# Rounded products of 384 and 192 columns for a hybrid decoder layer's second half of expert scores, and a reordered end

## Chip, core and metric

The kernel runs on one core of one Trainium2 chip. The metric is the device time of one launch in microseconds. Before the change it was 1906.36 us, the median of 3 runs (1906.03 to 1906.52).

## What is computed

One decoder layer on 256 tokens of width 2048, all in float32. A combined input projection feeds a retention group and a sparse attention group, whose joined output is projected and added to the residual. Then comes PEER, a layer of 16384 experts, and a final RMSNorm. PEER is what the change is about:

```python
def peer_ffn(x, wq, subkeys, u, v):
    ...
    def chunk(args):
        xc, ec, gc = args
        hid = jax.nn.gelu(jnp.einsum('cd,chkd->chk', xc, u[ec]))
        return jnp.einsum('chk,chkd->cd', gc * hid, v[ec])
    ...
    return out.reshape(B, T, D)
```

Each token has 128 chosen experts (8 heads of 16) with gates. `u` and `v` have 16384 rows of 2048.

## The kernel before

The program is one hand-written stream of instructions per engine, tied by semaphores. PE multiplies, ACT rounds and evaluates, DVE takes remainders and adds, POOL fetches rows by index, SP loads weight tiles.

**Dense and by pairs.** The first 192 tokens (`TD`) take the dense way: all 16384 experts are computed, in 128 blocks of 128 experts, and multiplied by a gate matrix that is zero for the experts not chosen. The last 64 tokens (`TS`) take only their own experts: 64 u items and 64 v items, each a gather of 128 rows of 8 KB by POOL (`fetch`, line 496) and one pass of DVE over them (`pair_item`, line 1535; lines 1554 and 1557). Between two items nothing but their place in DVE's stream sets the order: `STAGE_ITEMS` tells how many stand in which stretch of blocks, and POOL fetches `GATHER_LEAD` = 3 blocks ahead, into four buffers (`buffer_of`).

**Four stages.** The 128 blocks are worked in two halves of 64. A half has a u stage and a v stage.
- u stage (`u_block`, line 804): a tile of u, 128 x 2048, is loaded by SP into one of four slots of `raw`. PE multiplies its 16 slices of 128 columns by the 16 slices of `xn` (192 tokens), in full float32, line 813, into bank 0 or 1. ACT takes the gelu (line 1150) into `hidden`.
- v stage (`v_block`, line 890): a tile of v is split in two: ACT rounds it to `fp32r` in `hi` (line 1182, halves of 1024 columns), DVE takes the remainder in `lo` (line 1700). The gated hidden values are split likewise into `wm` (lines 1227, 1704, 1705). PE forms 20 products of 512 columns per block (lines 903 to 910) that add up in all eight banks: banks 0 to 3 for tokens 0 to 127, banks 4 to 7 for the other 64, whose rounded part and remainder are packed in one weight tile.
- In the second u stage banks 0 and 1 are wanted for u. So all eight banks are copied to `kept` by ACT (line 1232), stored to memory by POOL, and read back at the end.

In the first v stage the residual is added after the fourth block, by products with the identity: lines 941 (128 columns) and 943 (64 columns) in turn. At the end the 64 pair tokens (`acc`) and the two parts of tokens 128 to 191 are folded together by products with `fold_high` and `fold_low` (lines 956, 957), then come squares, sums, the root and the scaling (lines 1241, 1724, 983 to 985, 1728) in two tiles of 128 tokens.

**What waits for what in the second u stage.** PE's block waits for the tile's load and the gelu before last. SP's next load waits for PE's block. DVE works on pair items alone there. In the v stages SP's load waits for DVE's remainder, ACT's rounding for PE's use of the block two before (`hi` and `lo` have two buffers), DVE for ACT, PE for both.

## Time and profile before

| | us |
|---|---|
| median of 3 runs | 1906.36 |
| the profiled execution's own time | 1907.51 |
| its span, first to last instruction | 1905.7 |
| PE busy | 1872.8 (98%) |
| DVE busy | 1203.8 (63%) |
| ACT busy | 631.8 (33%) |
| DMA, mean | 279 GB/s |
| granted TensorE clock | 0.994 of full |

A group's mean is the time of one instruction from start to end. Products overlap, so the price of one is the time from one start to the next. A full float32 product shows as two instructions, a rounded one (`fp32r`) as one; the views print both as f32. The tables by stage give busy times of each engine in a stretch, with the count of instructions.

### The profile page before, as it was taken

Reading aid. Unit: us, or ns where it says so; the run is one execution under the profiler, and the core shown is the slowest. Engines: PE = TensorE matmul, PEld = TensorE weight load, DVE = VectorE, ACT = ScalarE, POOL = GpSimd, SP = SyncE. Lnnn points to the kernel's source line nnn. Section 1 sums busy time; section 2 is a strip of 40 time slices with the busy share of each in tenths; the row PEclk is TensorE's granted clock in tenths of the full one; section 3 lists DMA queues with packets and bytes.
Section 4 is the critical chain, followed back from the end, with each engine's and each line's share of the span. In section 5 each row is a group of like instructions: output and inputs, shape, how many; then the busy total and the mean of one; then the engine's idle time right before and its main releaser. Section 6 shows DMA issues by size and latency. Waiting matters only on the chain.

```text
span 1905.7 us, 29101 instructions
## 1 busy us (share of the span) xinstructions
PE 1872.8 (98%) x11564; PEld 1702.1 (89%) x11564; DVE 1203.8 (63%) x1929; ACT 631.8 (33%) x906; POOL 228.5 (12%) x151
## 2 busy tenths in 40 slices
PE   8999999998999999999999999999999999999997
PEld 8989999898999999999977777789999998777775
DVE  5535665566339696888457788844232225888885
ACT  5233445454331101111135555520000003555554
POOL 0000000000000111222101131312111112201400
PEclk9999999999999999999999999999999999999999
DMA  8774343455544898989879989879888988999884
GB/s 264 275 273 148 133 136 131 177 177 182 179 147 155 310 335 303 335 332 334 349 298 350 330 312 335 334 304 398 338 339 338 347 313 324 343 350 341 327 310 164
DMA packets 76144, 532.21 MB, mean 279 GB/s; under 512 B 8964, under 2 KB 9220, under 8 KB 15261
## 3 DMA queue, kind: packets, MB, share of 16 engines
q1 hardware_dynamic: 53280, 379.42, 54.0%
q0 software_dynamic: 22400, 151.07, 21.4%
q8 instruction: 52, 0.85, 0.2%
q10 hardware_dynamic: 380, 0.61, 0.1%
q14 instruction: 32, 0.25, 0.0%
HBM read 513.70 MB, written 17.30 MB: 279 GB/s over the span
## 4 chain that ended last, share of the span: by engine, by line
PE 98%; DVE 1%; ACT 0%; issue 0%; DMA 0%; DVEq 0%; ACTq 0%
PE bank L813 35%; PE bank L538 8%; PE bank L539 8%; PE bank L540 8%; PE bank L909 6%; PE bank L904 6%; PE bank L910 6%; PE bank L903 6%; PE bank L908 6%; PE bank L868 2%; PE bank L578 1%; PE bank L616 0%; PE bank L827 0%; PE bank L669 0%; PE bank L688 0%
## 5 line engine op out<-in xcount | busy, mean ns | idle before, releaser
L813 PE MATMUL bank<-hT,raw 128*128 128x192 f32 x4096 | 670.7, 326 | 1.3 <-ACT kept L1232 1.3
L813 PEld LDWEIGHTS bank<-hT,raw 128*128 128x128 f32 x4096 | 665.0, 190 | 2.0 <-issue 2.0
L1700 DVE TENSOR_TENSOR lo<-raw,hi 128x1024 fp32r<-128x1024 f32 x256 | 308.7, 1224 | 117.0 <-ACT hi L1182 116.8
L538 PE MATMUL bank<-act,hi 128*128 128x256 f32 x1216 | 354.3, 291 | 11.4 <-DVE act L1261 6.2
L1182 ACT ACTIVATE hi<-raw 128x1024 fp32r<-128x1024 f32 x256 | 270.6, 1060 | 273.2 <-PE bank L910 268.8
L539 PE MATMUL bank<-act,hi 128*128 128x256 f32 x1216 | 347.3, 286 | 0.0
L540 PE MATMUL bank<-act,lo 128*128 128x256 f32 x1216 | 347.1, 285 | 0.0
L1253 DVE TENSOR_TENSOR lo<-raw,hi 128x2048 fp32r<-128x2048 f32 x76 | 174.1, 2291 | 146.6 <-ACT hi L969 83.5
L538 PEld LDWEIGHTS bank<-act,hi 128*128 128x128 f32 x1216 | 236.5, 195 | 20.5 <-issue 19.2
L1150 ACT ACTIVATE arena<-bank 128x192 f32<-128x192 f32 x128 | 42.3, 330 | 591.4 <-PE bank L813 591.4
L539 PEld LDWEIGHTS bank<-act,hi 128*128 128x128 f32 x1216 | 236.6, 195 | 1.5 <-issue 1.4
L540 PEld LDWEIGHTS bank<-act,lo 128*128 128x128 f32 x1216 | 236.4, 194 | 0.0
L1557 DVE SCALAR_TENSOR_TENSOR acc<-rows_sb,wcol,acc 128x2048 f32<-128x2048 f32 x64 | 150.3, 2349 | 123.9 <-DMA rows_sb<-in_v,pairs 123.5
L1554 DVE SCALAR_TENSOR_TENSOR rows_sb<-rows_sb,xs 128x2048 f32<-128x2048 f32 x64 | 146.5, 2289 | 113.3 <-DMA rows_sb<-in_u_rows,pairs 113.1
L904 PE MATMUL bank<-lo,wm 128*64 128x512 f32 x512 | 202.6, 396 | 0.0
L909 PE MATMUL bank<-hi,wm 128*128 128x512 f32 x512 | 202.4, 395 | 0.0
L903 PE MATMUL bank<-hi,wm 128*128 128x512 f32 x512 | 199.3, 389 | 2.9 <-DVE wm L1705 2.9
L910 PE MATMUL bank<-hi,wm 128*128 128x512 f32 x512 | 200.9, 392 | 0.0
L908 PE MATMUL bank<-lo,wm 128*128 128x512 f32 x512 | 199.6, 390 | 0.0
L503 POOL DMA_INDIRECT rows_sb<-in_v,pairs x64 | 104.0, 1625 | 492.8 <-PE bank L910 186.5
L503 POOL DMA_INDIRECT rows_sb<-in_u_rows,pairs x64 | 105.7, 1651 | 444.5 <-PE bank L910 167.7
L908 PEld LDWEIGHTS bank<-lo,wm 128*128 128x128 f32 x512 | 96.2, 188 | 46.5
(258 smaller groups left out, 1564.6 us busy)
## 6 DMA issues: line engine op xcount, KB each, us to landing
raw<-in_u SPq DMA_DIRECT2D x128, 1024.0 KB, 6.1
raw<-in_v SPq DMA_DIRECT2D x128, 1024.0 KB, 7.3
raw<-in_w_in SPq DMA_DIRECT2D x44, 1024.0 KB, 5.4
raw<-in_w_out SPq DMA_DIRECT2D x16, 1024.0 KB, 5.2
raw<-in_wq SPq DMA_DIRECT2D x16, 1024.0 KB, 4.8
gate_matrix<-gs POOLq DMA_DIRECT2D x12, 768.0 KB, 12.3
gs<-gate_matrix SPq DMA_DIRECT2D x12, 768.0 KB, 9.1
raw<-in_cmp_w SPq DMA_DIRECT2D x8, 1024.0 KB, 4.9
```

Of the source, the lines that this page charges most:

```text
L503: pool.indirect_dma_start(rows_sb[b][:, :], None, (u_rows, v_rows)[kind == "v"], bass.IndirectOffsetOnAxis(ap=pair_rows[:, j:j + 1], axis= ...
L538: mm(dst, wh, mh, start=first, stop=False)
L539: mm(dst, wh, ml, start=False, stop=False)
L540: return mm(dst, wl, mh, start=False, stop=last)
L813: last = mm(bank[s % 2][:, 0:TD], raw[:, s, k * P:(k + 1) * P], xn[:, k, 0:TD], start=(k == 0), stop=(k == KT - 1))
L903: mm(bank[4 + dc][:, :], packed, vh[:, cols], start=opening, stop=False, skip_group_check=True)
L904: return mm(bank[4 + dc][0:TS, :], packed[:, 0:TS], vl[:, cols], start=False, stop=closing, skip_group_check=True)
L908: mm(bank[dc][:, :], whole, vl[:, cols], start=opening, stop=False, skip_group_check=True)
L909: mm(bank[dc][:, :], whole, vh[:, cols], start=False, stop=False, skip_group_check=True)
L910: return mm(bank[dc][:, :], rest, vh[:, cols], start=False, stop=closing, skip_group_check=True)
L1182: do(hi[:, s % 2, cols], raw[:, s, cols], ACT.Copy).then_inc(v_hi_ready, 1)
L1700: vec.tensor_tensor(lo[:, mv % 2, cols], raw[:, mv % RAW, cols], hi[:, mv % 2, cols].bitcast(F32), ALU.subtract).then_inc(v_lo_ready, 1)
```

## The change

- **Second u stage.** The tiles of u in the second half are split by ACT and DVE as those of v (`round_split`, `rest_split`), and `xn` too, into `xr`: 192 rounded columns and 192 of remainder per slice. A slice of 16 then takes two rounded products: `hi` by all 384 columns and `lo` by the 192 rounded ones (`REST_COLS`). They replace one full float32 product. Rounded times remainder stands in the bank's second 192 columns, so DVE adds the two (`sum_u`) and ACT's gelu works on the sum (`hidden_gelu`). The remainder of u times that of xn is left out, as it is in the v stages.
- `xr` is made in the first v stage, blocks 24 to 40, one slice a block on ACT and DVE (`spread_xn`, `spread_rest`). It takes the place of `xn` and of one gather buffer; from there on three buffers are used. `STAGE_ITEMS` has 27, 38 and 25 items for 26, 42 and 22.
- **Between the halves** banks 2 to 7 keep adding up through both halves; only banks 0 and 1 are copied (`kept`). Nothing goes to memory and back.
- **v blocks** form the products of tokens 128 to 191 of half a tile before those of tokens 0 to 127.
- **Residual.** All steps with 128 columns stand first, then those with 64 columns, alternately into the two halves of the banks' partitions.
- **End.** The pair tokens are finished by themselves during the last v blocks (POOL adds them with a DMA, ACT and DVE scale them). In the last block the products of tokens 128 to 191 come first, are copied by ACT and DVE and folded into 64 + 64 partitions by four products (`fold_second_tiles`) ahead of banks 2 and 3. One table of functions is loaded ahead for the logarithm and the exponential.

```diff
-def v_halves(half): return 2 * HALF * half
+SPLIT_0 = m_v(0)
+SPREAD_AT = 24
+REST_COLS = 192
...
-STAGE_ITEMS = ((PAIRS_LISTED, ROUTED, FIRST_GATHERS), (ROUTED, HALF - 4, 24), (HALF, 2 * HALF, 26),
-               (2 * HALF, 3 * HALF - 3, 42), (3 * HALF, 4 * HALF - 10, 22))
+STAGE_ITEMS = ((PAIRS_LISTED, ROUTED, FIRST_GATHERS), (ROUTED, HALF - 4, 24), (HALF, 2 * HALF, 27),
+               (2 * HALF, 3 * HALF - 3, 38), (3 * HALF, 4 * HALF - 10, 25))
...
-    return i % 2 if i < FIRST_GATHERS else 2 + i % 2 if items_by(HALF + 8) > i else i % 4
+    return i % 2 if i < FIRST_GATHERS else 2 + i % 2 if items_by(HALF + 8) > i else (0, 2, 3)[i % 3]
...
-        kept_back = at("kept_back", 40960, [P, 2 * D])
+        xr = at("xr", 22528, [P, KT, 2 * TD], F32R)
...
+        kept = [gs[:, x, 1536:2048] for x in range(2)]
...
+                if half:
+                    with sp.Fori(0, HALF // RAW) as lap:
+                        for s in range(RAW):
+                            load_after_v(a["u"][RAW * lap + (HALF + s)], 2 * RAW * lap + 2 * (HALF - RAW + s + 1), s)
...
+            def u_split_block(r, s, opening=False):
+
+                if opening:
+                    pe.wait_ge(half_kept, r + 1)
+                    pe.wait_ge(xr_lo, KT)
+                else:
+                    pe.wait_ge(u_summed, r - 1)
+                acc_bank = bank[s % 2]
+                for k in range(KT):
+                    if k % 8 == 0:
+                        pe.wait_ge(v_hi_ready, 2 * r + (2 * HALF + k // 8 + 1))
+                        pe.wait_ge(v_lo_ready, 2 * r + (2 * HALF + k // 8 + 1))
+                    w = slice(k * P, (k + 1) * P)
+                    mm(acc_bank[:, 0:2 * TD], hi[:, s % 2, w], xr[:, k, :], start=(k == 0), stop=False, skip_group_check=True)
+                    last = mm(acc_bank[:, 0:REST_COLS], lo[:, s % 2, w], xr[:, k, 0:REST_COLS], start=False, stop=(k == KT - 1),
+                              skip_group_check=True)
+                    if k == 7:
+                        last.then_inc(v_half_done, 1)
+                last.then_inc(block_done, 1)
+
...
+                        for part in range(2):
+                            split_loaded(part)
+                            for dc in (2 * part, 2 * part + 1):
+                                second_tile(dc)
+                            if opening and part == 0:
+                                if half:
+                                    pe.wait_ge(u_summed, HALF)
+                                else:
+                                    pe.wait_ge(acc_evacuated, M_PEER + HALF)
+                            for dc in (2 * part, 2 * part + 1):
+                                last = first_tile(dc)
+                                if closing and dc == 0:
+                                    last.then_inc(sums_done, 1)
+                            if part == 0:
                                 last.then_inc(v_half_done, 1)
                     last.then_inc(block_done, 1)
 
-
-                pe.wait_ge(acc_evacuated, M_PEER + HALF * (half + 1))
...
+                def fold_second_tiles():
+
+                    for dc in range(4):
+                        if dc % 2 == 0:
+                            pe.wait_ge(fold_even, dc // 2 + 1)
+                            pe.wait_ge(fold_odd, dc // 2 + 1)
+                        last = mm(bank[4 + dc // 2][TS * (dc % 2):TS * (dc % 2 + 1), :], fold_rows, fold_in[:, dc * 512:(dc + 1) * 512],
+                                  start=True, stop=True)
+                    last.then_inc(folded, 1)
...
-                            last = mm(bank[4 + dc][0:TS, j * P:(j + 1) * P], res_back[:, k * T + P:k * T + TD],
+                    for dc in range(4):
+                        for j in range(4):
+                            k, x = 4 * dc + j, j % 2
+                            last = mm(bank[4 + dc][TS * x:TS * (x + 1), j * P:(j + 1) * P], res_back[:, k * T + P:k * T + TD],
                                       ident, start=False, stop=False, skip_group_check=True)
...
+            def hidden_gelu(r):
+
+                ac.wait_ge(u_summed, r + 1)
+                cols = hidden[:, r * TD:(r + 1) * TD]
+                do(cols, cols, ACT.Gelu_apprx_tanh).then_inc(acc_evacuated, 1)
...
+            def round_split(n):
+
+                s, m = n % RAW, SPLIT_0 + n
+                ac.wait_ge(raw_loaded[s], 16 * ((m + 8) // RAW + 1))
                 for part in range(2):
...
-                    if part == 0 and mv >= 2:
-                        ac.wait_ge(v_half_done, (HALF - 1) * half + mv - 1)
+                    if part == 0 and n >= 2:
+                        ac.wait_ge(v_half_done, n - 1)
                     else:
-                        ac.wait_ge(block_done, m_v(half) + mv - 1)
...
+            def spread_xn(k):
+
+                if k == 0:
+                    ac.wait_ge(res_added, 1)
+                    ac.wait_ge(wm_lo, SPREAD_AT - 1)
+                if k >= 5:
+                    ac.wait_ge(xr_lo, min(k, math.ceil(1.5 * k - 6.5)))
+                src = xn_last[:, k - KT + 2, :] if k >= KT - 2 else xn[:, k, 0:TD]
+                do(xr[:, k, 0:TD], src, ACT.Copy).then_inc(xr_hi, 1)
...
+            def round_gated(half, mv):
+
+                weights = hidden[:, mv * TD:(mv + 1) * TD]
...
-                    for r in range(HALF):
-                        if r == HALF - 1:
-                            round_v(1, 0)
-                        hidden_block(1, r)
+                    for r in range(1, HALF):
+                        round_split(HALF + r)
+                        if r >= 2:
+                            hidden_gelu(r - 2)
...
+                    if half and mv == HALF - 6:
+
+                        nc.scalar.preload_act_table_set("natural_log_exp_and_others")
+                        ac.wait_ge(acc_folded, 16)
+                        do(squares[0:TS, 0:D], fin_third, ACT.Square, accum_out=small[0:TS, 8:9]).then_inc(fin_sq, 1)
+                        ac.wait_ge(fin_sq, 1)
+                        rsqrt(small[0:TS, 8:9], small[0:TS, 9:10], D, fin_log, fin_rstd, 1, rows=TS)
-                    ac.wait_ge(block_done, m_v(0) + HALF)
-                    for b in range(8):
-                        do(kept[:, b * 512:(b + 1) * 512], bank[b][:, :], ACT.Copy).then_inc(half_kept, 1)
...
+                    round_split(HALF)
+                    for x in range(2):
+                        if x == 0:
+                            ac.wait_ge(sums_done, 1)
+                        else:
+                            ac.wait_ge(v_half_done, HALF)
+                        do(kept[x], bank[x][:, :], ACT.Copy).then_inc(half_kept, 1)
...
+            def rest_split(n, part):
+
+                cols = slice(part * 1024, (part + 1) * 1024)
+                dv.wait_ge(v_hi_ready, 2 * n + part + 1)
+                vec.tensor_tensor(lo[:, n % 2, cols], raw[:, n % RAW, cols], hi[:, n % 2, cols].bitcast(F32),
+                                  ALU.subtract).then_inc(v_lo_ready, 1)
+
+            def sum_u(r):
+
+                dv.wait_ge(block_done, m_u(1) + r + 1)
+                vec.tensor_reduce(hidden[:, r * TD:(r + 1) * TD], bank[r % 2][:, 0:2 * TD].rearrange("p (a t) -> p t a", a=2),
+                                  AX.X, ALU.add).then_inc(u_summed, 1)
+
+            def spread_rest(k):
+
+                src = xn_last[:, k - KT + 2, :] if k >= KT - 2 else xn[:, k, 0:TD]
+                dv.wait_ge(xr_hi, k + 1)
+                vec.tensor_tensor(xr[:, k, TD:2 * TD], src, xr[:, k, 0:TD].bitcast(F32), ALU.subtract).then_inc(xr_lo, 1)
+
             for half in range(2):
                 if half:
-                    items_to(items_by(3 * HALF - 1))
-                    dv.wait_ge(half_stored, 16)
+                    for r in range(HALF):
+                        rest_split(HALF + r, 0)
+                        if r >= 2:
+                            sum_u(r - 2)
+                        rest_split(HALF + r, 1)
+                        items_to(items_by(2 * HALF + r - 1))
 
                 for mv in range(HALF):
...
+                    rest_split(2 * HALF * half + mv, 0)
+                    if half and mv < 2:
+                        sum_u(HALF - 2 + mv)
+                    rest_split(2 * HALF * half + mv, 1)
+                    if half == 0 and mv == SPREAD_AT - 2:
+                        for k in range(2):
+                            vec.tensor_copy(xn_last[:, k, :], xn[:, KT - 2 + k, 0:TD])
+                    if half == 0 and 0 <= mv - SPREAD_AT - 1 < KT:
+                        spread_rest(mv - SPREAD_AT - 1)
...
+            dv.wait_ge(fin_rstd, 1)
+            vec.scalar_tensor_tensor(out=fin_third, in0=fin_third, scalar=small[0:TS, 9:10], in1=norm_row[0:TS, :],
+                                     op0=ALU.mult, op1=ALU.mult).then_inc(fin_ready, 1)
+            for dc in (1, 3):
+                dv.wait_ge(sums_done, dc + 2)
+                vec.tensor_copy(fold_in[:, dc * 512:(dc + 1) * 512], bank[4 + dc][:, :]).then_inc(fold_odd, 1)
+            for dc in range(2):
+                dv.wait_ge(sums_done, dc + 6)
+                vec.tensor_tensor(fin_first[:, dc * 512:(dc + 1) * 512], bank[dc][:, :], kept[dc], ALU.add).then_inc(fin_added, 1)
```

**PE, from the last products of the first v stage to the second u stage.** `hT` holds `xn`. Before:

```order
L910 MATMUL bank<-hi,wm 128x512
L908 MATMUL bank<-lo,wm 128x512
L909 MATMUL bank<-hi,wm 128x512
L910 MATMUL bank<-hi,wm 128x512
L813 MATMUL bank<-hT,raw 128x192 x64
```

With the change:

```order
L935 MATMUL bank<-hi,wm 128x512
L933 MATMUL bank<-lo,wm 128x512
L934 MATMUL bank<-hi,wm 128x512
L935 MATMUL bank<-hi,wm 128x512
L835 MATMUL bank<-xr,hi 128x384
L836 MATMUL bank<-xr,lo 128x192
L835 MATMUL bank<-xr,hi 128x384
L836 MATMUL bank<-xr,lo 128x192
```

One kind of product of 192 columns, 16 a block, has become two kinds in turn, 16 of each.

**DVE, early in the second u stage.** Lines 1557 and 1554 (before) and 1648 and 1645 (now) are pair items. Before:

```order
L1557 SCALAR_TENSOR_TENSOR acc<-rows_sb_63,wcol,acc 128x2048 [waits rows_fetched3,acc_step]
L1554 SCALAR_TENSOR_TENSOR rows_sb_60,hcol<-rows_sb_60,xs 128x2048 [waits rows_fetched0]
L1554 SCALAR_TENSOR_TENSOR rows_sb_61,hcol<-rows_sb_61,xs 128x2048 [waits rows_fetched1]
L1554 SCALAR_TENSOR_TENSOR rows_sb_62,hcol<-rows_sb_62,xs 128x2048 [waits rows_fetched2]
L1554 SCALAR_TENSOR_TENSOR rows_sb_63,hcol<-rows_sb_63,xs 128x2048 [waits rows_fetched3]
L1547 TENSOR_TENSOR wcol<-hcol,pairs 128x4 [waits hcol_ready]
L1557 SCALAR_TENSOR_TENSOR acc<-rows_sb_60,wcol,acc 128x2048 [waits acc_step,rows_fetched0,acc_begun,wcol_ready]
L1557 SCALAR_TENSOR_TENSOR acc<-rows_sb_61,wcol,acc 128x2048 [waits rows_fetched1,acc_step]
L1694 TENSOR_TENSOR wmt<-arena,gs 128x192 [waits wm_lo,acc_evacuated,gate_loaded0,half_stored]
L1700 TENSOR_TENSOR lo<-raw,hi 128x1024 [waits v_hi_ready] x2
```

With the change:

```order
L1773 TENSOR_TENSOR lo<-raw,hi 128x1024 [waits v_hi_ready]
L1779 TENSOR_REDUCE arena<-bank 128x192 [waits block_done]
L1773 TENSOR_TENSOR lo<-raw,hi 128x1024 [waits v_hi_ready] x2
L1779 TENSOR_REDUCE arena<-bank 128x192 [waits block_done]
L1773 TENSOR_TENSOR lo<-raw,hi 128x1024 [waits v_hi_ready]
L1648 SCALAR_TENSOR_TENSOR acc<-rows_sb_59,wcol,acc 128x2048 [waits rows_fetched0,acc_step]
L1773 TENSOR_TENSOR lo<-raw,hi 128x1024 [waits v_hi_ready]
L1779 TENSOR_REDUCE arena<-bank 128x192 [waits block_done]
L1773 TENSOR_TENSOR lo<-raw,hi 128x1024 [waits v_hi_ready]
L1648 SCALAR_TENSOR_TENSOR acc<-rows_sb_61,wcol,acc 128x2048 [waits rows_fetched2,acc_step]
```

Items that stood in a row now stand between the remainders of u (line 1773) and the sums (line 1779), both of which PE waits for.

**PE, the residual after the fourth v block.** Before:

```order
L908 MATMUL bank<-lo,wm 128x512
L909 MATMUL bank<-hi,wm 128x512
L910 MATMUL bank<-hi,wm 128x512
L941 MATMUL bank<-base,res_back 128x128
L943 MATMUL bank<-base,res_back 64x128
L941 MATMUL bank<-base,res_back 128x128
L943 MATMUL bank<-base,res_back 64x128
```

With the change:

```order
L933 MATMUL bank<-lo,wm 128x512
L934 MATMUL bank<-hi,wm 128x512
L935 MATMUL bank<-hi,wm 128x512
L984 MATMUL bank<-base,res_back 128x128 x16
L989 MATMUL bank<-base,res_back 64x128 x16
L992 UNCONDITIONAL_BRANCH
```

The steps with 128 and with 64 columns of weights no longer alternate.

## Rows read from the trace of the kernel before

**Rows 1.** Page, part 4: share of the span in the chain that ended last.
```profile
PE 98%; DVE 1%; ACT 0%; issue 0%; DMA 0%; DVEq 0%; ACTq 0%
PE bank L813 35%; PE bank L538 8%; PE bank L539 8%; PE bank L540 8%; PE bank L909 6%; PE bank L904 6%; PE bank L910 6%; PE bank L903 6%; PE bank L908 6%; PE bank L868 2%; PE bank L578 1%; PE bank L616 0%; PE bank L827 0%; PE bank L669 0%; PE bank L688 0%
```

**Rows 2.** Busy time by stage: first v, second u, second v.
```profile
core 0: us, PE busy (x) PEld busy (x) DVE busy (x) ACT busy (x) POOL busy (x), PEclk, DMA share, GB/s
...
950.00:1257.00 307.00, 307.00 (x1340) 233.46 (x1339) 243.56 (x328) 148.13 (x191) 56.96 (x24) 1.00 0.89 324
1259.00:1593.00 334.00, 333.04 (x2048) 332.77 (x2048) 100.99 (x70) 26.96 (x81) 49.76 (x45) 1.00 0.88 342
1594.00:1889.00 295.00, 295.00 (x1280) 226.35 (x1280) 251.88 (x354) 148.95 (x193) 53.94 (x20) 1.00 0.86 321
```

**Rows 3.** Groups by line and shape, whole span (busy us, mean ns of one).
```profile
L1700 DVE TENSOR_TENSOR lo<-raw,hi 128x1024 fp32r<-128x1024 f32 x256 | 308.7, 1224 | 117.0 <-ACT hi L1182 116.8
L1182 ACT ACTIVATE hi<-raw 128x1024 fp32r<-128x1024 f32 x256 | 270.6, 1060 | 273.2 <-PE bank L910 268.8 <-DMA raw<-in_v 4.4
L1150 ACT ACTIVATE arena<-bank 128x192 f32<-128x192 f32 x128 | 42.3, 330 | 591.4 <-PE bank L813 591.4
L1557 DVE SCALAR_TENSOR_TENSOR acc<-rows_sb,wcol,acc 128x2048 f32<-128x2048 f32 x64 | 150.3, 2349 | 123.9 <-DMA rows_sb<-in_v,pairs 123.5
L1694 DVE TENSOR_TENSOR wmt<-arena,gs 128x192 f32<-128x192 f32 x96 | 52.4, 546 | 17.6 <-DMA gs<-gate_matrix 17.6
L1400 DVE SCALAR_TENSOR_TENSOR hT<-bank,gs 128x384 f32<-128x384 f32 x16 | 8.9, 557 | 3.3 <-PE bank L669 3.3
```

**Rows 4.** Chain that ended last, in order of time: start us, us, what.
```profile
562.34 7.14 PE bank L827 x64
...
578.53 3.65 PE bank L836 x64
...
968.64 0.36 PE bank L943 x2
969.01 0.42 PE bank L941 x2
...
1259.35 333.05 PE bank L813 x2048
```

**Rows 5.** Timeline of PE, two w_q products 24 apart, two L903 five apart, the last ones.
```profile
470.71 0.28 PE L539 MATMUL bank<-act,hi 128*128 128x256 f32 x1
...
473.57 0.28 PE L539 MATMUL bank<-act,hi 128*128 128x256 f32 x1
...
1882.14 0.39 PE L903 MATMUL bank<-hi,wm 128*128 128x512 f32 x1
...
1883.29 0.39 PE L903 MATMUL bank<-hi,wm 128*128 128x512 f32 x1
...
1888.79 0.39 PE L910 MATMUL bank<-hi,wm 128*128 128x512 f32 x1
```

**Rows 6.** Second u stage (1259 to 1593 us) in 40 slices: rate of all DMA.
```profile
GB/s 188 378 427 422 421 421 420 423 289 379 307 325 367 276 396 279 410 398 276 348 334 308 375 281 408 274 403 379 283 345 318 333 377 286 409 390 175 263 234 340
```

**Rows 7.** Waits of DVE in the same stage: us in total, times, longest us.
```profile
DVE acc L1557 <- DMA rows_sb<-in_v,pairs: 117.8, 22, 21.6
```

**Rows 8.** Timeline of PE, the first product of the stages (idle before it <- releaser).
```profile
949.75 0.47 PE L903 MATMUL bank<-hi,wm 128*128 128x512 f32 x1 [1.44 <-DVE wm L1705]
...
1259.35 0.40 PE L813 MATMUL bank<-hT,raw 128*128 128x192 f32 x1 [1.27 <-ACT kept L1232]
...
1593.82 0.47 PE L903 MATMUL bank<-hi,wm 128*128 128x512 f32 x1 [1.44 <-DVE wm L1705]
```

**Rows 9.** Timeline of the end of the kernel.
```profile
1896.09 0.60 ACT L1241 ACTIVATE arena<-bank 128x512 f32<-128x512 f32 x1 [0.35 <-PE bank L957]
...
1899.69 0.20 ACT L985 ACTIVATE small<-small 128x1 f32<-128x1 f32 x1
1899.93 2.73 DVE L1728 SCALAR_TENSOR_TENSOR arena<-bank,small,hT 128x512 f32<-128x512 f32 x4 [2.96 <-ACT small L985]
```

250 lines of the change are left out of this document (120 added, 130 removed).

## The prediction

> **What bounds the kernel now.** I read the chain that ended last first: 98% of the span is TensorE, 35% of it on line 813, the full float32 products of both u stages [rows 1]. So the time is what PE has to do, as long as its operands are there, and every price below is a time from one PE start to the next. The table by stage says the same for the two v stages and the second u stage: PE is busy in practically all of each [rows 2]. The reader is to see in it that the engines beside PE are very unlike: DVE is at 79% and 85% in the v stages, but at 30% in the second u stage (100.99 of 334.00 us), and ACT at 8%. The clock there is granted in full (1.00). The chain in order of time then gives the u stage its price: 333.05 us for 64 blocks of 16 products, 1024 in all, so 0.325 us a product of 192 columns [rows 4]. PE's timeline gives the price of a rounded product (one instruction each): 24 of 256 columns from 470.71 to 473.57, so 0.119 us; five of 512 columns from 1882.14 to 1883.29, so 0.230 us [rows 5].
>
> The sum is made against the profiled execution's own 1907.51 us (span 1905.7); the median of the runs shown is 1906.36, 1.15 less, which I take off at the end.
>
> **The u stage, PE.** Of 1024 products at 0.325 us become 1024 of 384 columns and 1024 of 192, all rounded. The first lies between two measured sizes: the line through 256 and 512 columns rises 0.111 us in 256 columns, so 384 cost 0.119 + 0.0555 = 0.1745 us. No rounded product under 256 columns stands in this trace, so the second is bounded from both sides. Below: the same line drawn on, 0.119 - 0.028 = 0.091 us. Above: the full float32 price of the same 192 columns, 0.325 us. I take neither. A product of 192 columns is so short that loading its 128 columns of weights may take longer. The nearest row for that is line 827, 64 instructions with loads of 128 columns in 7.14 us, 0.1116 each; with loads of 64 columns into alternating halves (line 836) the same count takes 3.65 us [rows 4]. So 0.1116 us, since the only thing in the new product unlike the 256-column one is its width, and nothing in the rows makes a rounded product dearer when it is narrower. Per weight tile 0.1745 + 0.1116 = 0.286 us, times 1024 = 293 us: **40.2 us less** than 333.05.
>
> The Trainium skill states another rule, in "TensorE: Matmul & The Clock Gate", section "Back-to-back issue gap": a product follows the last after its columns over 2.4 GHz plus 2.5 ns. The trace disagrees at both widths it has, 216 ns by the Trainium skill against 230 [rows 5] for 512 columns and 109 against 119 for 256. By the Trainium skill alone the pair would be 162.5 + 82.5 = 245 ns and PE's share of the stage 251 us. What that would make of the time is the rival of the unburdened narrow product below.
>
> **The u stage, what must now keep up.** The stage's u tiles are now rounded by ACT and the remainder taken by DVE, as in the v stages, and DVE adds the two halves of a bank before ACT's gelu.
> - DVE per block: two remainders, 308.7/256 = 1.206 us each [rows 3], 2.41; the sum, which reads 384 columns from a bank, at least 0.33 (ACT's copy-like pass over 192) and at most about 0.7 (half as much again as the nearest); I take the nearest row, line 1400 with 384 columns from a bank, 0.557; and 38 pair items in 64 blocks at 2.35 [rows 3], 1.40. Together 4.37 us, 280 us for the stage, beside PE's 4.58 and 293. That is 95% and the closest cover in this forecast. If PE were faster than 280 us, DVE would hold it.
> - ACT per block: two roundings at 1.06 and a gelu at 0.33 [rows 3], 2.45 us of 4.58. Costs nothing.
> - The rounded and remainder tiles have two buffers each. ACT may start a block's first half only when PE has used half of the block two before. So a remainder may come 1.5 blocks, 6.9 us, after its buffer is free; it takes 1.06 + 1.21, and at most one item (2.35) and one sum (0.56) stand ahead of it: 5.2 us. It fits, without much room. Nothing queued on ACT behind the new wait for the sum is late by more than the sum itself.
> - DMA: 64 tiles and 38 gathers of 1.05 MB are 107 MB (now 64 and 42, in 333 us). In 293 us that is 365 GB/s. The stage runs at 342 now [rows 2], but slices of it at 421 to 427 [rows 6], so the rate exists. SP's loads now wait for the remainder and not for PE's block; the remainder comes earlier, so a load is issued no later.
>
> **The v stages.** In the first, 16 slices of xn are rounded by ACT and their remainders taken by DVE: 16 x 0.33 = 5.3 us on ACT, 18 x 0.546 = 9.8 us [rows 3] and one item more, 2.35, on DVE. It goes from 243.6 to about 256 of 307 us [rows 2]: covered. In the second, three items more (7 us) on 251.9 of 295: covered. If that cover were gone, all of it, some 19 us, would be on the path. Gathers have three buffers for four; POOL fetches about 4.5 blocks ahead, an item comes every 1.6 blocks or more, so a buffer is free when the fetch is due. The second tile's products stand ahead of the first tile's; that moves nothing in the sum, since PE issues the same 20 per block.
>
> **Adding the residual.** Now each 128-column step is followed by a 64-column one on line 943: 0.36 + 0.42 us a pair [rows 4], 16 such pairs, 12.5 us. Afterwards all of line 941's kind come first, 32 instructions at 0.1116 (line 827), and then 32 with 64-column loads that alternate between two halves, as line 836's do, 3.65/64 = 0.057 us. 3.6 + 1.8 = 5.4 us: **7.1 us less**. Unless the residual's layout, and not the alternation, makes these steps slow; then nothing.
>
> **Three joints.** PE stood 1.27 us for ACT's copy of a bank between the halves and 1.44 us for DVE's wm before each v stage, at 949.75 and 1593.82 [rows 8]. Afterwards a bank's copy begins while the last v block still runs, only two banks are copied, and a v block opens with products that need no u result. 1.27 + 2 x 1.44 = **4.1 us less**.
>
> **The end.** Now the last product starts at 1888.79 [rows 5] and the span ends at 1905.7, 16.9 us. The 64 pair tokens are finished before, and the half sums are not brought back. What stays behind the last product: its 0.39, a square 0.8 with its read, a sum 0.2 and two small steps of 0.2 to 0.3 each with their hand-overs, 0.8, scaling four 512-wide pieces 2.73, two more 1.4 [rows 9], and the last DMA, which now takes the 3.0 us from 1902.7 to the end. That is 9.4 us, 7.5 less, also because one table for both small steps is loaded ahead. Against it stand four folding products ahead of the last six: between 1.7 us, if their halves run beside each other, and 3.4; I take 2.5. **5.0 us less**. The new waits of the fold, on ACT's and DVE's copies of 0.6 to 0.7 us, lie under six products of 0.23.
>
> **Sum.** 1907.5 - 40.2 - 7.1 - 4.1 - 5.0 = 1851.1, less 1.15: **1850 us**.
>
> **Rivals.**
> - *The narrow product keeps its full float32 price* (ends slower). For it: the trace has no rounded product under 256 columns, while all 192-column products of the u stages cost 0.325; if the array gives the rounded rate only from some width on, the narrow product pays this. Against it: between 512 and 256 columns the price falls nearly in step with the width. Pair 0.1745 + 0.325 = 0.500 us, stage 512 us, 179 more: 1907.5 + 178.6 - 16.2 - 1.2 = 2069. It decides from a narrow product of 0.167 us on: there the pair costs 0.341 and the stage's loss of 16 us eats the 16.2 gained elsewhere. DVE would idle, with 8.0 us a block to fill.
> - *Half of that*: one float32 instruction of the two, 0.163. Stage 345, 12 more: 1902, not to be told from no change.
> - *DVE's waits for gathers take the stage.* Now DVE stands up to 21.6 us for a gather in this stage, 117.8 us in all for line 1557's [rows 7], at no cost, since nothing PE needs is behind it. Now remainders are. If the loads and gathers keep to the stage's 342 GB/s, its 107 MB take 313 us: 20 less than now and not 40, 1870. Against: most of those waits come from DVE running ahead of the fetches, which items now placed after each block can't.
> - *The narrow product isn't held by its weights* (the rule of the Trainium skill is one form of it). At 0.091 PE needs 272 us, under DVE's 280, which then holds: 1907.5 - 53 - 16.2 - 1.2 = 1837.
> - That the change doesn't do what it says is no rival: the order of PE's instructions shows both widths alternating.
>
> **Chances.** The forecast 0.56; narrow product unheld 0.13; gather waits 0.13; float32 price 0.15; half of it 0.03. A measurement of this kernel tells 0.2% (3.8 us) from no change. Faster by more: 0.82; within: 0.03; slower: 0.15. The range takes in the rivals at 1837 and 1870 with the bounds of their costs (the residual's 7 us either way, DVE's sum at 0.33 to 0.7, 10 us a side): 1828 to 1880. It leaves out the float32 price and its half, 0.18.
>
> **What would show it.** In the profile after: a start-to-start of 0.11 us for the narrow product (line 836 of the changed kernel) beside 0.17 for the wide one (its line 835), a stage of 64 blocks in 293 us with DVE over 90% busy; the residual in 5 to 6 us; no idle over 0.5 us at the joints; 10 us from the last product to the end, the fold aside. Wrong it is if the narrow one's is above 0.15, if DVE's idle in the stage is put down to gathers, or if PE waits for the remainders (its line 1773) block by block.

## The result, and the profile after

The changed kernel takes 1846.12 us, the median of 4 runs (1845.95 to 1846.27); the kernel before took 1906.34 beside it (1906.03 to 1906.52). The ratio is 0.9684, with a 95% interval of 0.9667 to 0.9701. The profiled execution has 1846.27 us and a span of 1844.5, 61.2 us less than before. The mean granted TensorE clock is 0.994 in both.

The page of the kernel after, its span, busy times and chain (as [rows 1]):

```profile
span 1844.5 us, 29701 instructions
...
PE 1815.4 (98%) x11560; PEld 1654.8 (90%) x11560; DVE 1380.4 (75%) x2133; ACT 764.3 (41%) x1043; POOL 162.5 (9%) x151
...
PE 97%; DVE 1%; ACT 0%; issue 0%; DMA 0%; DVEq 0%; ACTq 0%
PE bank L819 18%; PE bank L835 11%; PE bank L548 8%; PE bank L549 8%; PE bank L550 8%; PE bank L929 6%; PE bank L928 6%; PE bank L933 6%; PE bank L934 6%; PE bank L935 6%; PE bank L836 5%; PE bank L894 2%; PE bank L588 1%; PE bank L626 0%; PE bank L853 0%; PE bank L679 0%
```

PE still sets the time. The float32 products, now line 819, have fallen from 35% of the span to 18%; the two rounded ones (835 wide, 836 narrow) take 16%. DVE has gone from 63% to 75%, with nothing of it on the chain to speak of.

The table by stage, for the first v stage, the second u stage and the second v stage (as [rows 2]; stretch, length, busy us and count of PE, PEld, DVE, ACT, POOL, clock, DMA share, GB/s):

```profile
947.00:1246.80 299.80, 298.91 (x1344) 231.27 (x1343) 251.76 (x349) 157.91 (x215) 28.16 (x28) 1.00 0.94 341
1246.90:1538.00 291.10, 291.10 (x2048) 291.10 (x2047) 266.98 (x258) 154.40 (x196) 41.79 (x37) 1.00 0.96 369
1538.00:1834.00 296.00, 295.76 (x1290) 226.62 (x1289) 258.10 (x358) 154.85 (x204) 26.00 (x25) 1.00 0.89 326
```

The second row is the change's heart: 2048 products in 291.10 us, PE never idle, DVE at 92% of it where it had 30%, DMA at 369 GB/s where it had 342. PE's timeline shows the joint to the second u stage and, far inside it, the steady pair (start, us, engine and line; as [rows 5] and [rows 8]):

```profile
1246.67 0.39 PE L935 MATMUL bank<-hi,wm 128*128 128x512 f32 x1
1246.89 0.33 PE L835 MATMUL bank<-xr,hi 128*128 128x384 f32 x1
...
1300.26 0.25 PE L836 MATMUL bank<-xr,lo 128*128 128x192 f32 x1
1300.26 0.19 PEld L835 LDWEIGHTS bank<-xr,hi 128*128 128x128 f32 x1
1300.34 0.36 PE L835 MATMUL bank<-xr,hi 128*128 128x384 f32 x1
1300.37 0.19 PEld L836 LDWEIGHTS bank<-xr,lo 128*128 128x128 f32 x1
1300.54 0.25 PE L836 MATMUL bank<-xr,lo 128*128 128x192 f32 x1
1300.54 0.19 PEld L835 LDWEIGHTS bank<-xr,hi 128*128 128x128 f32 x1
```

The joint is 0.22 us from start to start, a product's usual price. A pair takes 1300.54 - 1300.26 = 0.28 us; over the stage, 291.25/1024 = 0.2844. The recorded starts of the products split it as 0.08 for the narrow one and 0.20 for the wide; the starts of the loads (PEld) split it as 0.11, from the load of line 835 to that of line 836, and 0.17 to the next one of line 835. Which product pays for what the two don't tell alike, and the experiments had to. The other thing to see is when a load starts: the wide product's weights (line 835) begin to load when the narrow one before it starts, no sooner.

The groups that answer to [rows 3], and the passes over gathered rows (as [rows 7]):

```profile
L1773 DVE TENSOR_TENSOR lo<-raw,hi 128x1024 fp32r<-128x1024 f32 x384 | 463.7, 1221 | 113.0 <-ACT hi L1232 112.5
L1232 ACT ACTIVATE hi<-raw 128x1024 fp32r<-128x1024 f32 x384 | 404.8, 1059 | 325.8 <-PE bank L935 236.3 <-PE bank L836 82.9 <-DMA raw<-in_v 6.2
...
L1648 DVE SCALAR_TENSOR_TENSOR acc<-rows_sb,wcol,acc 128x2048 f32<-128x2048 f32 x64 | 150.2, 2347 | 8.9 <-DMA rows_sb<-in_v,pairs 8.3
...
L1779 DVE TENSOR_REDUCE arena<-bank 128x192 f32<-128x384 f32 x64 | 35.2, 550 | 0.0
```

Line 1773 has 384 instructions for 256: a third stage is split. The sum of a bank's halves (1779) takes 0.550 us. DVE's idle before the passes of line 1648 for a gather has gone from 123.5 us to 8.3. The waits inside the second u stage are short (engine and line, waited for: total us, times, longest):

```profile
POOL rows_sb L513 <- DVE acc L1648: 120.2, 19, 8.6
...
ACT hi L1232 <- PE bank L836: 81.7, 88, 1.2
ACT arena L1200 <- DVE arena L1779: 41.2, 44, 2.5
DVE lo L1773 <- ACT hi L1232: 23.8, 47, 1.2
```

PE waits for nothing in this stage, and DVE waits for ACT's rounding alone, by half a microsecond a time. POOL waits for DVE now to free a buffer; DVE never waits for POOL's gathers.

Stage by stage, from the first PE start of one to that of the next, in us:

| | before | after | difference | forecast |
|---|---|---|---|---|
| up to the first u product | 557.0 | 555.5 | -1.4 | 0 |
| first u stage, joint | 392.8 | 391.0 | -1.7 | -1.4 |
| first v stage, joint | 309.6 | 300.3 | -9.3 | -8.4 |
| second u stage, joint | 334.5 | 291.3 | -43.2 | -41.6 |
| second v stage, with the fold | 295.0 | 295.9 | +0.9 | +2.5 |
| last product's start to the end | 16.9 | 10.45 | -6.5 | -7.5 |
| sum (rounded parts) | 1905.7 | 1844.5 | -61.2 | -56.4 |

The chain in order of time shows the residual (as [rows 4]):

```profile
965.19 3.57 PE bank L984 x32
968.76 1.90 PE bank L989 x32
970.66 0.42 PE bank L928
```

3.57 + 1.90 = 5.47 us, where it was 12.5. And the timeline of the end (as [rows 9]; in brackets the idle time before and what ended it):

```profile
1831.81 1.03 PE L972 MATMUL bank<-arena,base 128*64 128x512 f32 x4
...
1834.05 0.39 PE L935 MATMUL bank<-hi,wm 128*128 128x512 f32 x1
...
1834.47 0.60 ACT L1317 ACTIVATE arena<-bank 128x512 f32<-128x512 f32 x1
...
1835.38 0.29 ACT L1027 ACTIVATE small<-small 128x1 f32<-128x1 f32 x1 [0.22 <-DVE small L1838]
1835.71 0.20 ACT L1029 ACTIVATE small<-small 128x1 f32<-128x1 f32 x1
...
1837.12 0.61 PE L1000 MATMUL bank<-small,base 128*128 128x1 f32 x4 [2.69 <-ACT arena L1317]
...
1838.60 1.40 DVE L1846 SCALAR_TENSOR_TENSOR arena<-bank,small,hT 128x512 f32<-128x512 f32 x2
1840.02 1.50 SPq L481 DMA_DIRECT2D out<-arena  x2
```

No loading of a table stands between the two small steps (1027 and 1029). PE's last work is to add up the other tile's squares at 1837.12, and after DVE's last scaling 4.5 us go by to the end of the span.

### The profile page after: what moved, and what is told of

Its sections match the earlier page's. It is cut to its first block, busy times and chain, and to the rows that moved or that the text cites. A ratio compares the mean times of both kernels' runs of the same rounds, so it can differ in the third digit from the quotient of the medians.

```text
span 1844.5 us, 29701 instructions
## 1 busy us (share of the span) xinstructions
PE 1815.4 (98%) x11560; PEld 1654.8 (90%) x11560; DVE 1380.4 (75%) x2133; ACT 764.3 (41%) x1043; POOL 162.5 (9%) x151
## 4 chain that ended last, share of the span: by engine, by line
PE 97%; DVE 1%; ACT 0%; issue 0%; DMA 0%; DVEq 0%; ACTq 0%
PE bank L819 18%; PE bank L835 11%; PE bank L548 8%; PE bank L549 8%; PE bank L550 8%; PE bank L929 6%; PE bank L928 6%; PE bank L933 6%; PE bank L934 6%; PE bank L935 6%; PE bank L836 5%; PE bank L894 2%; PE bank L588 1%; PE bank L626 0%; PE bank L853 0%; PE bank L679 0%
## 5 line engine op out<-in xcount | busy, mean ns | idle before, releaser
L1773 DVE TENSOR_TENSOR lo<-raw,hi 128x1024 fp32r<-128x1024 f32 x384 | 463.7, 1221 | 113.0 <-ACT hi L1232 112.5
L1232 ACT ACTIVATE hi<-raw 128x1024 fp32r<-128x1024 f32 x384 | 404.8, 1059 | 325.8 <-PE bank L935 236.3
L819 PE MATMUL bank<-hT,raw 128*128 128x192 f32 x2048 | 337.6, 326 | 0.0
L819 PEld LDWEIGHTS bank<-hT,raw 128*128 128x128 f32 x2048 | 332.2, 190 | 0.3 <-issue 0.3
L835 PE MATMUL bank<-xr,hi 128*128 128x384 f32 x1024 | 291.3, 359 | 0.0
L836 PE MATMUL bank<-xr,lo 128*128 128x192 f32 x1024 | 256.3, 250 | 0.0
L836 PEld LDWEIGHTS bank<-xr,lo 128*128 128x128 f32 x1024 | 195.6, 191 | 0.0
L835 PEld LDWEIGHTS bank<-xr,hi 128*128 128x128 f32 x1024 | 191.8, 187 | 0.0
```

The lines of the kernel that those rows point to most:

```text
L819: last = mm(bank[s % 2][:, 0:TD], raw[:, s, k * P:(k + 1) * P], xn[:, k, 0:TD], start=(k == 0), stop=(k == KT - 1))
L835: mm(acc_bank[:, 0:2 * TD], hi[:, s % 2, w], xr[:, k, :], start=(k == 0), stop=False, skip_group_check=True)
L836: last = mm(acc_bank[:, 0:REST_COLS], lo[:, s % 2, w], xr[:, k, 0:REST_COLS], start=False, stop=(k == KT - 1), skip_group_check=True)
L1232: do(hi[:, s % 2, cols], raw[:, s, cols], ACT.Copy).then_inc(v_hi_ready, 1)
L1773: vec.tensor_tensor(lo[:, n % 2, cols], raw[:, n % RAW, cols], hi[:, n % 2, cols].bitcast(F32), ALU.subtract).then_inc(v_lo_ready, 1)
```

## The experiments

Each starts from the kernel after and changes what its diff shows. The expectations number the theories. The first is the forecast's own: a narrow product is held to 0.1116 us by a load of 128 weight columns. The others are what speaks against it: that the price follows the width, or that a rounded product grows dear below some width. Beside the three groups of runs the kernel before took 1906.78, 1906.54 and 1906.62 us. The first u product starts between 555.2 and 556.3 us in kernels that are alike up to there, so the length of a stage tells more than a total.

### What does the narrow product's price depend on?

**Its width: 256, 128 and 64 columns.** With 128 or 64, the tokens above that number go without the product of u's remainder; with 256, 64 tokens gain the product of both remainders, which the kernel leaves out. The edit for 256, the other two alike:

```
-REST_COLS = 192
+REST_COLS = 256
```

> The changed kernel with narrow products of 256 columns instead of 192; the 64 extra columns add a term of remainder times remainder that is left out otherwise. Measured so far: a pair of wide and narrow product takes 0.285 us, 292 us a stage, 1846.1 us in all. Theory 1, the 192-column product is held by the load of its 128 columns of weights (0.111 us) and costs nothing for its columns: at 256 columns it costs what such products cost in the w_q stage, 0.119, the pair 0.2935, the stage 8.7 us more, 1855 us. Theory 2, the pair is paid by its columns at 0.434 ns each: 28 us more, 1874. Theory 3, narrow products are dear under some width between 192 and 256: the pair gets cheaper or stays.

> The changed kernel with narrow products of 128 columns; this leaves out the product of u's remainder for tokens 128 to 191. Theory 1 (held by the weight load): 0.111 us as before, no change, 1846 us. Theory 2 (paid by columns): 28 us of PE less, PE at 264 us a stage; DVE was busy 267 us in it and would then hold at 270 to 280: 1826 to 1836 us. Theory 3 (narrow products are dear under some width): twice the price of a float32 instruction of 128 columns, 0.223 us, the pair 0.40, 115 us more: 1961.

> The changed kernel with narrow products of 64 columns; this leaves out the product of u's remainder for tokens 64 to 191. Theory 1 (held by the weight load): no change, 1846 us. Theory 2 (paid by columns): PE at 235 us a stage, DVE holds at 270 to 280: 1826 to 1836 us. Theory 3: the pair above 0.29 us, slower than 1850.

Measured: 256 columns 1856.17 us (ratio 0.9735, 0.9719 to 0.9751), stage 300.4; 128 columns 1848.82 (0.9696, 0.968 to 0.9713), stage 293.5; 64 columns 1849.98 (0.9702, two runs only), stage 293.5; and 192, the kernel after, 291.2. So a product of 256 columns costs 9.2/1024 = 0.009 us more than one of 192, about as far as 0.119 is above 0.1116, and below 192 nothing is gained: the pair goes from 0.2844 to 0.2866, slightly up. Below the 0.11 us, whatever sets them, the width is free. That speaks against both other theories at once: if the price followed the width, a product of 64 columns would save 10 to 20 us, as far as DVE lets it; if narrow products grew dear, the pair would take 0.29 us and more. Both kernels are slower than the 1846 us that the weight load alone had them at, by 2.7 and 3.9 us, of which 2.2 lie in this stage. PE's timeline at 256 columns:

```profile
1300.09 0.28 PE L836 MATMUL bank<-xr,lo 128*128 128x256 f32 x1
1300.21 0.34 PE L835 MATMUL bank<-xr,hi 128*128 128x384 f32 x1
1300.38 0.28 PE L836 MATMUL bank<-xr,lo 128*128 128x256 f32 x1
```

0.12 and 0.17: the price of 256 columns and, within the 0.01 us of these starts, the 0.1745 that the forecast's line gives 384; nothing is held. The two prices make 0.2935, and the stage has 300.4/1024 = 0.2934.

**Its own load: 64 weight columns.** Only half of the experts of a tile get their remainder.

```
-                    last = mm(acc_bank[:, 0:REST_COLS], lo[:, s % 2, w], xr[:, k, 0:REST_COLS], start=False, stop=(k == KT - 1),
+                    last = mm(acc_bank[0:TS, 0:REST_COLS], lo[:, s % 2, k * P:k * P + TS], xr[:, k, 0:REST_COLS], start=False, stop=(k == KT - 1),
```

> The changed kernel with narrow products of 192 columns, but with only 64 columns of weights, so that the load is half as long; this leaves out u's remainder for half of the experts of a block. Theory 1 (the 192-column product is held by the load): the load falls to 0.057 us and the product costs its columns, 0.091; the pair 0.266, PE 272 us a stage instead of 292; DVE, busy 267 us there, is nearly the bound: stage 272 to 282 us, 1826 to 1836 us. Theory 2 (not the load): no change, 1846 us.

Measured: 1845.39 us (0.9678, 0.9662 to 0.9694), the stage 290.1 us, 1.1 less than the kernel after. Theory 1, as worded, missed (1826 to 1836): a narrow product with half the load costs practically what it did. Either the load had never held it, and some other floor of 0.11 us did, or the load that holds it is another one. The timeline of the kernel after points to the second: while the narrow product runs, the weights that are being loaded are those of the *next wide* product. The narrow one's own were loaded under the wide one before it, which lasts 0.1745 us and covers them. So the edit had halved a load that was hidden.

**The wide product's load: 64 weight columns.** The counterpart. Half of the experts of a tile get no rounded part of u; the work of every other engine is kept. The edit halves the outputs of the wide product as well as its load; the same halving of the narrow product, just now, brought 1 us.

```
-                    mm(acc_bank[:, 0:2 * TD], hi[:, s % 2, w], xr[:, k, :], start=(k == 0), stop=False, skip_group_check=True)
+                    mm(acc_bank[0:TS, 0:2 * TD], hi[:, s % 2, k * P:k * P + TS], xr[:, k, :], start=(k == 0), stop=False, skip_group_check=True)
```

> The changed kernel with only 64 columns of weights in the wide product (384 columns), the narrow product whole; this leaves out most of the scores of half the experts of a block. Halving the narrow product's own load changed nothing (pair 0.284 us). Theory 1, corrected: a load runs while the product before it runs, so what the narrow product waits out is the load of the next wide product, 128 columns, 0.111 us. Halved it is 0.057, less than the narrow product's 0.091: pair 0.266, PE 272 us a stage; DVE was busy 267 us and nearly holds it: stage 272 to 282 us, 1827 to 1837 us. Rival: the pair has a fixed price of its own that no load sets: no change, 1846 us.

Measured: 1832.98 us (0.9613, 0.9598 to 0.9628), the stage 278 us. PE's timeline:

```profile
1300.03 0.25 PE L836 MATMUL bank<-xr,lo 128*128 128x192 f32 x1
1300.03 0.13 PEld L835 LDWEIGHTS bank<-xr,hi 128*64 128x64 f32 x1
1300.12 0.34 PE L835 MATMUL bank<-xr,hi 128*64 128x384 f32 x1
1300.12 0.19 PEld L836 LDWEIGHTS bank<-xr,lo 128*128 128x128 f32 x1
1300.30 0.25 PE L836 MATMUL bank<-xr,lo 128*128 128x192 f32 x1
```

The row of that stage in the table by stage, and then PE's wait for DVE among the waits:

```profile
1246.80:1524.80 278.00, 274.56 (x2050) 272.83 (x2049) 265.55 (x258) 149.82 (x196) 42.02 (x37) 1.00 0.98 384
```

```profile
PE bank L835 <- DVE arena L1779: 3.2, 5, 1.0
```

A pair now takes 0.27 us (0.266 over five of them), which is 0.1745 + 0.091, the price the forecast gave a narrow product that nothing holds. The same product, with the same weights of its own, costs 0.09 or 0.11 us by what is loaded behind it. This split of the pair is worked out from the price of 384 columns; what is measured is that the pair is 0.018 us shorter. The row of the table shows the next two bounds coming near: DVE is at 96% and DMA's share at 0.98, and PE begins to wait for DVE's sum, 3.2 us in all.

The Trainium skill, in "TensorE: Matmul & The Clock Gate", section "Back-to-back issue gap", gives columns over 2.4 GHz plus 2.5 ns for a product taken by itself, and says that this comes out too low for few columns, because it leaves no time for the weight load. By it the pair would take 245 ns. Neither run agrees: 284 ns with the load in the way and 266 without.

**The order: two wide, then two narrow.** If the loads for both narrow products could be made under the wide ones, or the load of a wide one earlier, the narrow ones would not be held.

```
+                    for j in (k, k + 1):
+                        w = slice(j * P, (j + 1) * P)
+                        mm(acc_bank[:, 0:2 * TD], hi[:, s % 2, w], xr[:, j, :], start=(j == 0), stop=False, skip_group_check=True)
+                    for j in (k, k + 1):
+                        w = slice(j * P, (j + 1) * P)
+                        last = mm(acc_bank[:, 0:REST_COLS], lo[:, s % 2, w], xr[:, j, 0:REST_COLS], start=False, stop=(j == KT - 1),
+                                  skip_group_check=True)
```

> The changed kernel with the products of two slices in the order wide, wide, narrow, narrow. Corrected theory 1 (one load ahead and no more): each narrow product still has a load of 128 columns to wait out, two pairs take 2 x 0.1745 + 2 x 0.111: no change, 1846 us. Rival (loads can run further ahead, and only the turning between widths costs): 20 ns a pair less, PE at 272 us a stage, 1827 to 1837 us.

PE's timeline (838 is the wide product here, 841 the narrow one; a row holds two):

```profile
1300.06 0.36 PE L841 MATMUL bank<-xr,lo 128*128 128x192 f32 x2
1300.26 0.54 PE L838 MATMUL bank<-xr,hi 128*128 128x384 f32 x2
1300.64 0.36 PE L841 MATMUL bank<-xr,lo 128*128 128x192 f32 x2
```

Measured: 1848.65 us (0.9692), the stage 293.5. Two pairs take 1300.64 - 1300.06 = 0.58 us; over the stage a pair takes 0.2866, 0.002 more than in turn, which is not explained, and not 0.02 less. In either order a narrow product has one load of 128 columns behind it and costs 0.11. If loads could be made further ahead, that of the second narrow product would be done under the wide ones, and at least the first narrow one would not be held. So here only one load is made ahead.

### What does DVE's cover amount to?

**The sum three times over** in 60 of the 64 blocks, the two extra results going nowhere.

```
+                if r < HALF - 4:
+                    vec.tensor_reduce(spare[(r + 0) % 3], bank[r % 2][:, 0:2 * TD].rearrange("p (a t) -> p t a", a=2),
+                                  AX.X, ALU.add)
+                    vec.tensor_reduce(spare[(r + 1) % 3], bank[r % 2][:, 0:2 * TD].rearrange("p (a t) -> p t a", a=2),
+                                  AX.X, ALU.add)
```

> The changed kernel with the sum of a bank's halves taken three times by DVE in 60 of the 64 blocks of the second u stage, twice into spare memory. DVE is busy 267 of 291 us there. If that cover is as thin as its busy time says: 60 x 2 x 0.46 to 0.55 us more are 55 to 66, DVE at 322 to 333 us sets the stage, 31 to 42 us more: 1877 to 1888 us. If DVE's work hides at no such limit (PE doesn't wait for it): 1846 us.

A stretch of 322 us inside the stage in the table by stage, and the waits of PE and DVE in it (1786 is the sum here):

```profile
1248.00:1570.00 322.00, 294.51 (x1974) 288.22 (x1974) 310.55 (x364) 140.52 (x187) 40.85 (x36) 0.98 0.89 321
```

```profile
PE bank L835 <- DVE arena L1786: 27.4, 30, 2.4
...
DVE lo L1773 <- ACT hi L1232: 11.3, 27, 1.2
```

Measured: 1888.56 us (0.9903), the stage 333.3 us, 42 more. DVE is busy for 321 us of it, where it was 267: the 120 extra sums are 54 us of busy time, 0.45 each, and not 66, because one starts 0.46 to 0.47 us after the last though it lasts 0.55. Of the 54 us, 12 were covered and 42 are the stage's growth; of DVE's 24 idle microseconds 12 are left, waits for ACT's rounding. So DVE sets the stage at 96% busy, and PE waits for the sum 30 times in some 62 blocks.

The growth is not all waiting: PE waits for 27.4 us. Its four longest waits, 1.87 to 2.42 us (they end at 1312.64, 1381.38, 1446.12 and 1514.87), are followed within 2 us by slices with a granted clock of 0.50, the lower of the clock's two levels. From 1313.92 to 1314.45 a pair takes 0.53 us there instead of 0.284, and the kernel after has 1.00 over the whole stage. How much of the 42 us this makes was not measured by a run of its own.

### What is the rest of the change worth?

**The second u stage in full float32 again**, ACT's roundings, DVE's remainders and sums and the items all kept. DVE's sum reads the one half that is left twice. Because PE reads `raw` again, SP's loads in this stage wait for PE's block, as before, and no longer for DVE's remainder; the lines below are PE's only.

```
-                    mm(acc_bank[:, 0:2 * TD], hi[:, s % 2, w], xr[:, k, :], start=(k == 0), stop=False, skip_group_check=True)
-                    last = mm(acc_bank[:, 0:REST_COLS], lo[:, s % 2, w], xr[:, k, 0:REST_COLS], start=False, stop=(k == KT - 1),
+                    last = mm(acc_bank[:, 0:TD], raw[:, s, w], xr[:, k, 0:TD].bitcast(F32), start=(k == 0), stop=(k == KT - 1),
```

> The changed kernel with one full float32 product of 192 columns in the second u stage instead of the two rounded ones; all else of the change stays, the splitting of u by ACT and DVE and the sum too. The product works on the rounded part of xn and the sum counts it twice, so the hidden values of that half are not those of the reference. If the rounded pair is the whole gain of the stage and the rest of the change is worth the other 18 us: stage 333 instead of 292 us, 1846 + 41 = 1887 us. If the added work of DVE and ACT costs something of its own in the float32 stage: above 1890.

Measured: 1887.56 us (0.99, 0.9884 to 0.9917), the stage 333 us again. The products, with that wait of SP, are worth 41.4 us, everything else 19.

**The residual in turn**, as before: a 128-column step, then a 64-column one, all into the lower half of the partitions.

```
-                            k = 4 * dc + j
+                            k, x = 4 * dc + j, 0
...
-                    for dc in range(4):
-                        for j in range(4):
-                            k, x = 4 * dc + j, j % 2
```

> The changed kernel with the residual's products in the order of before: a step with 128 columns of weights, then one with 64, in turn, the latter always into the lower 64 partitions. If the turning between the two sizes of load is what made these steps slow: they take 12.5 us instead of the 5.5 measured with the change, 7 us more, 1853 us. If not (the residual's layout, or the memory it comes from): they stay at about 5.5, 1846 us.

**The residual grouped, but on one side**: the 64-column steps no longer alternate between halves. The fold adds both halves, so all of it may go into one.

```
-                            k, x = 4 * dc + j, j % 2
+                            k, x = 4 * dc + j, 0
```

> The changed kernel with the residual's products grouped by size, but all 64-column ones into the lower 64 partitions. If alternating halves lets two run beside each other: without it 32 instructions at 0.107 to 0.112 us take 3.5 us instead of 1.9, 1.6 us more, 1847.7 us. If the halves don't matter: 1846.1 us.

The chain in order of time, first in turn (986 has the 64 columns here, 984 the 128), then on one side:

```profile
966.75 0.36 PE bank L986 x2
967.12 0.42 PE bank L984 x2
967.54 0.36 PE bank L986 x2
```

```profile
965.81 3.57 PE bank L984 x32
969.38 3.64 PE bank L989 x32
```

Measured: in turn 1853.8 us (0.9721), first v stage 307.5 us against 300.3; on one side 1849.11 (0.9706; 1848.13 to 1854.1), stage 302.1. In the profiled executions the stage also starts later than in the kernel after, by 1.0 and 0.6 us. Of the 7.1 us that taking turns costs, 5.4 come back by grouping, 1.7 by alternating between halves. With 64 columns of weights into the half that is in use an instruction costs 3.64/32 = 0.114 us, no less than one with 128 (0.1116). So in these steps it is not the weight load that sets 0.11. They are full float32 with 128 columns to multiply by; at line 819's price, 0.325/2 us for 192 columns, those alone make 0.108 us, an estimate.

**No table loaded ahead** for the end.

```
-                        nc.scalar.preload_act_table_set("natural_log_exp_and_others")
```

> The changed kernel without the table load ahead of the end. If the loads were a part of the old end's length: logarithm and exponential load a table each (1.28 us) in both of the last roots, two loads or more on the path, 2.6 to 5.1 us more, 1848.7 to 1851.2 us. If the loads fall into waits: under 1 us more.

The timeline of its end:

```profile
1836.35 1.28 ACT L1027 ACT_TABLE_LOAD   x1
...
1837.96 1.28 ACT L1029 ACT_TABLE_LOAD   x1
...
1840.66 1.01 PE L1000 MATMUL bank<-small,base 128*128 128x1 f32 x4 [5.05 <-ACT arena L1316]
```

Measured: 1851.81 us (0.9713). Two of the four loads of 1.28 us are in the first tile's way, two in the second's. From the last product to the end it is 14.4 us against 10.45; another 1.1 us lie in the second v stage, in front of its last product, where PE waits 1.3 us for ACT's rounding, once. The median is 0.6 us above the upper end of what was expected.

**The last tile's output by two queues.** Stores are issued piece by piece by SP and ACT rather than at the end by SP alone.

```
+            for c in range(2):
+                ac.wait_ge(fin_ready, 6 + c)
+                nc.scalar.dma_start(out[P:P + TS, c * 1024 + 512:(c + 1) * 1024], fin_second[TS:P, c * 512:(c + 1) * 512]).then_inc(out_stored, 16)
```

> The changed kernel with the last rows written in four pieces, each as soon as it is scaled, half of them issued by ACT beside SP. Between DVE's last scaling and the end lie 4.5 us, two transfers issued 0.75 us apart. If the issue and the wait for both pieces are part of it: 0.7 to 1.5 us less, 1844.6 to 1845.4 us. If the last transfer's own time is all: no change, 1846.1 us.

Measured: 1845.56 us (0.9678, 0.9665 to 0.9691), 0.6 less than the kernel after, with ranges that overlap (1845.25 to 1846.26 here, 1845.95 to 1846.27 there). After DVE's last scaling 3.7 us go by to the end instead of 4.5, and from the last product's start 9.7 instead of 10.45. So the stretch that the edit touches is 0.7 us shorter, the low end of what was expected; the total hardly tells it from nothing.

## Why the prediction was right, point by point

The forecast was 1850 us in a range of 1828 to 1880; measured are 1846.1. Of the 4.8 us by which the span fell further than the sum, 1.4 lie ahead of the first u product, where the change has nothing; among the changed kernels that start moves by 1.0 us by itself. The second u stage and the second v stage gave 1.6 us each more than forecast, the end 1.0 less, the first u and the first v stage 1.2 together.

- **The u stage.** Forecast 0.286 us a pair and 293 us, measured 0.2844 and 291.2. Both terms stand: 384 columns at 0.1745, as the run with 256 beside it shows, and a floor of 0.11 for the narrow product, which the widths 64, 128 and 192 show to be no matter of width. Two things in the working of that floor were wrong, and the number came out right by luck. It named the wrong load: it said that a product of 192 columns is so short that loading *its* weights takes longer. It is the load for the product behind it. In this kernel both have 128 columns, so the number was the same; an edit built on the wording, halving the narrow one's load, brought 1 us of the 10 to 20 it seemed to promise, and halving the other one brought 13. And it took 0.1116 from line 827, full float32 products of 128 columns, as the price of a load. Such an instruction costs about as much by its columns (0.108, the estimate above), and costs 0.114 with half the load, as the residual on one side shows. So that row did not tell the two apart; that a load of 128 columns takes 0.11 us is seen in the changed kernel, where the next load starts 0.11 us after it.
- **The other engines keep up.** DVE's single durations add up to about what was forecast (remainders 157, sums 35, items 90 in that stage: 282 for 280), but instructions overlap a little, and it is busy for 267 of 291 us, 92% and not 95%. It is idle for 24 us, of which the three sums a block could use 12. Remainders, waited for by PE block by block, had been named as a sign that the working is wrong; there is no such wait.
- **The gathers' rival** (1870) fell: DMA moved 369 GB/s where 342 had been seen over the stage, and DVE waits for no gather in it. The waits of [rows 7] are gone with the items spaced by the blocks, as argued against that rival; no run here put the items back in a row.
- **The float32 price for narrow products** (2069), and half of it, fell with the first pair of the trace. Down to 64 columns no rounded product here costs more than 0.112 us; the rate of those under 192 columns is hidden under the load.
- **The unheld narrow product** (1837) did not happen, and could be made to: with the load behind it halved, the pair costs what this rival had, 0.266, and the kernel 1833. DVE didn't hold it at 280 us, since it is busy for only 266; it cost 3 us of waits.
- **The residual.** 7.1 us forecast, 7.0 measured, and put back by taking turns again (7.1). Grouping carried 5.4 of it and the alternation between halves 1.7.
- **The joints.** 4.1 us forecast. In the trace after, 1.27 and 1.44 of them have gone wholly; 0.5 us are left before one v block, a wait for DVE's wm. The first v stage is about 1 us shorter beyond residual and joint; its cause was not traced.
- **The end.** 5.0 us forecast, 5.5 measured (6.5 less 0.9, from the unrounded parts). The fold cost 1.87 us where 2.5 were taken: its halves do run nearly side by side (8 instructions, 0.23 each, where one of the same 512 columns cost 0.43 in the old fold). Behind the last product it is 10.45 us and not 9.4, and 4.5 of them, after the last scaling, were taken for 3.0. Without the table loaded ahead the span is 5.1 us longer, 3.9 of them behind the last product.

## What to carry to other kernels

A rounded product of few columns costs at least as much as the load for the *next* product, 0.11 us here for 128 weight columns: below about 240 columns (an estimate, where the line through 256 and 512 meets 0.11) a narrower product gains nothing, and to make it faster one shrinks what is loaded behind it, not what it uses. Before work moves to another engine, add up its instructions for a block against PE's block and then look at its busy time in that stage, not the mean over the span: DVE made PE wait not at all at 92% of the stage, for 3 us at 96%, and at 96% with three sums a block it set the stage. A share of busy time alone doesn't say which. Once PE waits, look at the granted clock too: there the four longest waits were each followed by a stretch at half of it. Where full float32 steps with 128 and with 64 columns of weights mix, group them by size, and let the small ones alternate between halves of the array; in the rounded u stage mixing cost nothing. And take a price from a row in which only one cause can have set it.

## What was not expected of the hardware

The residual's steps with loads of 128 and 64 columns in turn cost 0.21 and 0.18 us an instruction, against 0.1116 and, between alternating halves, 0.059 when they are grouped. In the u stage the same two sizes in turn cost nothing extra (0.28 and 0.27 us a pair), so it isn't the change of size alone; the residual's products are full float32, the u stage's rounded, and which of that, or of the alternation between banks, makes it dear stays open. A narrow product of 128 or 64 columns made the pair 0.002 us dearer than one of 192, as did the order of two and two, and the narrow product's half load made it 0.001 cheaper; all of it is unexplained. The first u stage, in full float32 still, was not tried in rounded parts: `xr` takes the place of buffers that are in use there.
